# Seven adaLN modulation chunks of a two-layer diffusion step: weighted row sums on VectorE, TensorE only sums over partitions

## The reference

```python
def ada_modulation(cond, w, b):
    mod = jax.nn.silu(cond) @ w + b          # cond: 1024, w: 1024 x 6144
    return [m[:, None, :] for m in jnp.split(mod, 6, axis=-1)]

def modulate(h, shift, scale):
    return h * (1.0 + scale) + shift

# per layer: shift, scale, gate of the mixer, then of the experts
h = modulate(rmsnorm(x, norm_mix[layer]), sh_a, sc_a)
q, k, v = jnp.split(h @ nat_w_qkv[j], 3, axis=-1)      # layer 1
out = neighbourhood_attention(q, k, v, k_cache, v_cache, rpb) @ nat_w_o[j]
x = x + g_a * out
h = modulate(rmsnorm(x, norm_ffn[layer]), sh_f, sc_f)
x = x + g_f * grouped_moe(h, ...)
```

## Time and profile before

| what | value |
|---|---|
| median of 3 runs | 1315.08 us (1310.66 to 1315.25) |
| the profiled execution, whole | 1315.46 us |
| its span, first to last instruction | 1313.6 us |
| granted TensorE clock, mean over the span | 0.989 of full |
| busy: TensorE / VectorE / ScalarE / GpSimd | 1249.4 / 592.7 / 332.7 / 222.7 us |
| modulation matmuls (line 804), all | 1536 instructions, 64 a chunk |
| loads of modulation chunks by SyncE | 24, 2048 KB each |

### The profile page before, as it was taken

The page is one execution under the profiler, slowest core; times in us unless marked ns, Lnnn a source line. Parts: engine busy times, 40 slices in busy tenths (PEclk is TensorE's granted clock), DMA queues, the critical chain, the costliest instruction groups (busy, mean ns, idle before and its releaser), DMA issues.

```text
span 1313.6 us, 20008 instructions
## 1 busy us (share of the span) xinstructions
PE 1249.4 (95%) x7839; PEld 722.0 (55%) x7839; DVE 592.7 (45%) x1514; ACT 332.7 (25%) x785; POOL 222.7 (17%) x298
## 2 busy tenths in 40 slices
PE   5899999999999999999989999999999998999995
PEld 3665466666645654444444455555885455444442
DVE  5221266556535664444452000002883666444446
ACT  4121355445412400000032000002882340000002
POOL 6220500100100012122220100013221001222220
PEclk8999999999999999999989999999999999999998
DMA  9612411221574469999880363135326336999966
GB/s 382 222 41 81 175 66 66 80 116 66 209 270 170 161 240 374 377 375 381 326 262 16 141 229 129 65 142 195 92 58 245 146 129 246 376 378 378 375 182 192
DMA packets 45453, 267.87 MB, mean 204 GB/s; under 512 B 6980, under 2 KB 13460, under 8 KB 31520
## 3 DMA queue, kind: packets, MB, share of 16 engines
q1 hardware_dynamic: 22672, 192.85, 37.6%
q0 software_dynamic: 16928, 52.77, 14.3%
q10 hardware_dynamic: 5760, 20.97, 4.1%
HBM read 230.19 MB, written 34.81 MB: 202 GB/s over the span
## 4 chain that ended last, share of the span: by engine, by line
PE 85%; DVE 5%; DMA 5%; issue 3%; ACT 2%; POOL 0%; POOLq 0%; ACTq 0%; SPq 0%; DVEq 0%
PE PS L1175 14%; PE PS L915 13%; PE PS L1281 11%; PE PS L1129 10%; PE PS L1192 7%; PE PS L782 5%; PE PS L1046 5%; PE PS L788 4%; PE PS L1086 3%; PE PS L804 3%; PE PS L1340 2%; DMA xrows<-big 2%; PE PS L996 2%; PE PS L1303 1%; DMA big<-hrows,big 1%
## 5 line engine op out<-in xcount | busy, mean ns | idle before, releaser
L1129 PE MATMUL PS<-weights,ht 128*128 128x512 f32 x320 | 142.4, 596 | 1.0 <-DVE ht L1683 1.0
L1281 PE MATMUL PS<-ht,weights 128*128 128x128 f32 (+1 forms) x512 | 139.8, 434 | 0.0
L915 PE MATMUL PS<-weights,ht 128*128 128x336 f32 (+1 forms) x320 | 116.7, 523 | 1.6 <-ACT ht L1465 1.6
L1175 PE MATMUL PS<-big 128*128 128x512 f32 x256 | 113.1, 593 | 0.5 <-DVE big L2137 0.5
L1281 PEld LDWEIGHTS PS<-ht,weights 128*128 128x128 f32 x512 | 77.7, 191 | 62.1 <-issue 62.1
L782 PEld LDWEIGHTS PS<-const,big 128*128 128x128 f32 (+2 forms) x627 | 77.0, 144 | 58.1 <-issue 39.6
L782 PE MATMUL PS<-const,big 128*128 128x128 f32 (+2 forms) x627 | 92.3, 283 | 13.6 <-DVE big L1759 4.2
L1593 ACT ACTIVATE big<-PS 128x256 f32<-128x256 f32 x34 | 13.0, 383 | 337.1 <-PE PS L1175 337.1
L1129 PEld LDWEIGHTS PS<-weights,ht 128*128 128x128 f32 x320 | 59.0, 190 | 68.2 <-issue 68.2
L915 PEld LDWEIGHTS PS<-weights,ht 128*128 128x128 f32 x320 | 60.5, 191 | 52.8 <-issue 38.7
L1175 PE MATMUL PS<-weights,big 128*128 128x512 f32 x192 | 84.4, 592 | 0.0
(11 more groups left out here) (256 smaller groups left out, 1817.1 us busy)
## 6 DMA issues: line engine op xcount, KB each, us to landing
weights<-in_ada SPq DMA_DIRECT2D x22, 2048.0 KB, 8.7
big<-in_gu SPq DMA_DIRECT2D x16, 2048.0 KB, 22.7
weights<-in_gu SPq DMA_DIRECT2D x12, 2048.0 KB, 24.2
rows<-in_down SPq DMA_DIRECT2D x18, 1024.0 KB, 12.0
weights<-in_down SPq DMA_DIRECT2D x16, 1024.0 KB
ht<-in_gu SPq DMA_DIRECT2D x6, 2048.0 KB, 24.0
weights<-in_qkv SPq DMA_DIRECT2D x6, 2048.0 KB, 10.7
weights<-in_wo SPq DMA_DIRECT2D x4, 2048.0 KB, 8.9
```

The lines of the kernel that those rows point to most:

```text
L915: ins = pe.matmul(bank(4 + u % 2, n), lhs(k), rhs(k), start=(k == 0), stop=(k == ks - 1))
L1129: ins = pe.matmul(bank(4 + j), OT[:, k, t * P:(t + 1) * P], w[j][:, k, :], start=(k == 0), stop=(k == KD - 1))
L1175: ins = pe.matmul(bank(0), gatT[:, k, :], w[:, k, :], start=(k == 0), stop=(k == KD - 1))
L1281: ins = pe.matmul(bank(bb, n1 - n0), w[:, k, m * P:(m + 1) * P], hT[:, k, n0:n1], start=(k == 0), stop=(k == KD - 1))
```

## The change

Chunks 5 to 11 of the second layer are computed in another way. VectorE reads the chunk's weights (`ada_sums`): for each block k and each of the two conditioning vectors c it multiplies the 128 x 512 block by the per-partition scalar `condT[:, 2k+c]` and adds it to accumulator `acc[c]` (two places of 512 columns in `R`). That is 2 tensor_scalar and 14 scalar_tensor_tensor a chunk; each counts `m_acc`, and each waits for the operation before the last one. TensorE (`ada_summed`) then sums over the partitions: for both c and four groups a product with a two-column selector of constants (`C_PICK`), 8 products where there were 32. The buffer of a chunk's weights is free when VectorE has finished, no longer when TensorE has.

ScalarE takes all evictions of the v units from the second on, of the transposed keys and of the q/k units; VectorE keeps v unit 1. The places of the chunks move: 5 and 6 after v units 5 and 8, 7 to 11 after q/k units 2, 4, 6, 9 and 11. The order of the loads follows. All seven chunks use weight buffer 0. The bias tables come behind the eighth load (n == 7), which is chunk 7.

```diff
--- before.py
+++ after.py
...
@@ -102,6 +103,7 @@
     c[:, C_I16:C_I16 + E] = np.arange(E)
     c[:, C_E128:C_E128 + E] = np.arange(E) * P
     c[:, C_X9:C_X9 + XTILES] = np.arange(XTILES)
+    c[:, C_PICK:C_PICK + 3] = [1, 0, 1]
     c[:, C_EPS] = EPS
     c[:, C_EVEN:C_EVEN + 4] = [2, 4, 6, 8]
     c[:, C_FREE:C_FREE + 5] = [11, 15, 17, 19, 21]
@@ -194,6 +196,7 @@
         Pm = [[R[:, 3456 + (2 * i + j) * 640:3456 + (2 * i + j + 1) * 640] for j in range(2)] for i in range(2)]
         PTm = [R[:, 0:1408], rt[:, 0:1408]]
         ckc = R[:, 5376:5632]
+        acc = [R[:, 4864 + c * 512:4864 + (c + 1) * 512] for c in range(2)]
         ropet = rt[:, 0:1024].rearrange("p (n h x i) -> p n h x i", n=4, h=H, x=2)
 
         qT = big(0, 5120, KD)
@@ -288,6 +291,7 @@
         r_ab = sem("rows_in")
         r_g = sem("gates_in")
 
+        m_acc = sem("ada_sums_on_dve")
         m_mm, m_b, m_cp, m_st, m_tr, m_md = (sem(f"ada_{n}") for n in ("products", "bias_in", "rows", "stored", "transposed", "columns"))
         w_in = [sem(f"w_in{i}") for i in range(5)]
         w_half = sem("w_in3_second_half")
@@ -295,7 +299,7 @@
         g_mm, g_ea, g_ed = (sem(f"products_{x}") for x in ("done", "taken_act", "taken_dve"))
         AT_MM = {"win": 0, "uq": 10, "wo0": 42, "vproj": 52, "wo1": 62}
         AT_EA = {"win": 0, "uq": 5, "vproj": 21}
-        AT_ED = {"win": 0, "uq": 5, "wo0": 21, "vproj": 31, "wo1": 36}
+        AT_ED = {"win": 0, "uq": 5, "wo0": 21, "vproj": 31, "wo1": 32}
         l_sd, l_rs, l_n, l_tr, l_ta, l_td, l_rope, l_qr, k_rc = (sem(n) for n in (
             "lat_sqrt", "lat_rstd", "lat_normed", "lat_transposed", "lat_T_act", "lat_T_dve",
             "k_rope_ready", "q_rope_ready", "krope_copied"))
@@ -305,7 +309,7 @@
         ORDER = (CTX, 0, 1, 2, 3)
         NW = H // 2 * NT
         QK = tuple(range(8, 16)) + tuple(range(8))
-        ADA_QK = (3, 6, 9, 12)
+        ADA_QK = (2, 4, 6, 9, 11)
         WIN = ((0, 0), (1, 0), (0, 1), (1, 1), (2, 0), (2, 1), (3, 0), (3, 1), (4, 0), (4, 1))
         PV = 512 + 256
 
...
@@ -342,11 +346,11 @@
         FRONT = (0, 2, 1, 3)
         LOADS = [[("ada", 0, j) for j in FRONT] + [("win", 0, 0), ("win", 0, 1), ("uq", 0, 0), ("uq", 0, 1), ("ukv", 0, 0)]
                  + [("ada", 0, j) for j in range(4, 12)] + [("wo0", 0, 0), ("wo0", 0, 1)] + [("ada", 1, j) for j in range(4)],
-                 [("ada", 1, 4), ("qkv", 0, 4), ("qkv", 0, 5), ("ada", 1, 5), ("ada", 1, 6), ("ada", 1, 7)] + [("qkv", 0, 2), ("qkv", 0, 3)]
-                 + [("ada", 1, 8), ("ada", 1, 9), ("qkv", 0, 0), ("ada", 1, 10), ("ada", 1, 11), ("qkv", 0, 1), ("wo1", 0, 0), ("wo1", 0, 1)]]
+                 [("ada", 1, 4), ("qkv", 0, 4), ("qkv", 0, 5), ("ada", 1, 5), ("ada", 1, 6), ("qkv", 0, 2), ("qkv", 0, 3), ("ada", 1, 7), ("ada", 1, 8),
+                  ("qkv", 0, 0), ("ada", 1, 9), ("ada", 1, 10), ("qkv", 0, 1), ("ada", 1, 11), ("wo1", 0, 0), ("wo1", 0, 1)]]
 
         SLOTS_ = [[0, 1, 2, 3, 0, 1, 2, 0, 2] + [0, 1] * 4 + [0, 1] + [2] * 4,
-                  [4, 1, 2, 0, 0, 0, 1, 2, 0, 0, 1, 0, 0, 2, 0, 2]]
+                  [4, 1, 2, 0, 0, 1, 2, 0, 0, 1, 0, 0, 2, 0, 0, 2]]
 
         def in_columns(i):
 
@@ -389,6 +393,8 @@
 
         def products_done(what, l, j):
 
+            if what == "ada" and l and j > 4:
+                return m_acc, 16 * (j - 4)
             if what == "ada":
                 return m_mm, l * 12 + (FRONT.index(j) if l * 12 + j < 4 else j) + 1
             if what == "ukv":
@@ -551,7 +557,7 @@
                     sp.wait_ge(c_in[2], 16)
                     for n in range(2, len(LOADS[1])):
                         static_load(1, n)
-                        if n == 8:
+                        if n == 7:
                             sp.wait_ge(s_toepd, 16)
                             sp.wait_ge(c_in[NT - 1], 16)
                             sp.wait_ge(c_sum, 1)
...
@@ -805,6 +810,18 @@
                                         w[:, k, g * P:(g + 1) * P], start=(k == 0), stop=(k == KD - 1))
                 ins.then_inc(m_mm, 1)
 
+            def ada_summed(j):
+
+                i = 12 + j
+                pe.wait_ge(m_cp, i - 1)
+                pe.wait_ge(m_acc, 16 * (i - 16))
+                for c in range(2):
+                    pick = const[:, C_PICK + c:C_PICK + c + 2]
+                    for g in range(4):
+                        ins = pe.matmul(PS[32 * g:32 * g + 2, ada_out_at(i):ada_out_at(i) + P], pick,
+                                        acc[c][:, g * P:(g + 1) * P], start=(c == 0), stop=(c == 1))
+                ins.then_inc(m_mm, 1)
+
             def mod_transpose(i):
 
                 pe.wait_ge(m_cp, i + 1)
@@ -906,7 +923,9 @@
 
             def gemm_unit(name, u, n, ks, lhs, rhs, done=None):
 
-                if u >= 2:
+                if name == "vproj" and u >= 4:
+                    pe.wait_ge(g_ea, AT_EA[name] + u - 2)
+                elif u >= 2:
                     if u % 2 == 0:
                         pe.wait_ge(g_ea, AT_EA[name] + u // 2)
                     else:
@@ -1258,8 +1277,8 @@
                     x_transposes("m1", u + 2)
                 if u == 0:
                     last_part(0, 4)
-                if u in (5, 7, 9):
-                    ada(1, 5 + (5, 7, 9).index(u))
+                if u in (5, 8):
+                    ada_summed(5 + (5, 8).index(u))
 
             pe.wait_ge(kc_in, 32)
             for c in range(KD):
@@ -1271,9 +1290,8 @@
                     w = w_(w_wait(pe, "qkv", 0, u // 4), KD, 512)
                 if n == 1:
                     pe.wait_ge(kc_ta, 1)
-                    pe.wait_ge(kc_td, 1)
                 if n >= 2:
-                    pe.wait_ge(qk_ea if n % 2 == 0 else qk_ed, n // 2)
+                    pe.wait_ge(qk_ea, n - 1)
                 b = (2, 0)[n % 2]
                 m = u % 4
                 for n0, n1, bb in ((0, 512, b), (512, 640, b + 1)):
@@ -1281,10 +1299,9 @@
                         ins = pe.matmul(bank(bb, n1 - n0), w[:, k, m * P:(m + 1) * P], hT[:, k, n0:n1], start=(k == 0), stop=(k == KD - 1))
                 ins.then_inc(qk_mm, 1)
                 if n in ADA_QK:
-                    ada(1, 8 + ADA_QK.index(n))
+                    ada_summed(7 + ADA_QK.index(n))
                 if n == 8:
-                    pe.wait_ge(qk_ea, 4)
-                    pe.wait_ge(qk_ed, 4)
+                    pe.wait_ge(qk_ea, 8)
                     for c in range(KD):
                         ins = transpose(bank(4, P, c * P), kT[:, c, 512:640])
                     ins.then_inc(kc_tr, 1)
...
@@ -1621,7 +1636,7 @@
             def v_out(u):
                 act.wait_ge(g_mm, AT_MM["vproj"] + u + 1)
                 t, j = WIN[u]
-                act.activation(nv[:, t, j * 512:(j + 1) * 512], bank(4), ACT.Copy).then_inc(g_ea, 1)
+                act.activation(nv[:, t, j * 512:(j + 1) * 512], bank(4 + u % 2), ACT.Copy).then_inc(g_ea, 1)
 
             for t in range(NT + 1):
                 if t < NT:
@@ -1636,18 +1651,18 @@
                     ins.then_inc(n_ta, 1)
                 if t == 3:
                     v_out(0)
-            for u in (2, 4, 6, 8):
+            for u in range(2, 10):
                 v_out(u)
             act.wait_ge(kc_tr, 1)
-            act.activation(kcT[:, 0:4, :], bank(0).rearrange("p (c n) -> p c n", c=4), ACT.Copy).then_inc(kc_ta, 1)
-            for n in range(0, 16, 2):
+            act.activation(kcT[:, :, :], bank(0, D).rearrange("p (c n) -> p c n", c=KD), ACT.Copy).then_inc(kc_ta, 1)
+            for n in range(16):
                 act.wait_ge(qk_mm, n + 1)
                 u = QK[n]
                 dst = qT[:, u, :] if u < 8 else kT[:, u - 8, :]
-                act.activation(dst, bank(2, 640), ACT.Copy, scale=-NAT_SCALE if u < 8 else 1.0).then_inc(qk_ea, 1)
+                act.activation(dst, bank((2, 0)[n % 2], 640), ACT.Copy, scale=-NAT_SCALE if u < 8 else 1.0).then_inc(qk_ea, 1)
                 if n == 8:
                     act.wait_ge(kc_tr, 2)
-                    act.activation(kout[:, 0:512], bank(4), ACT.Copy).then_inc(kc_ta, 1)
+                    act.activation(kout, bank(4, D), ACT.Copy).then_inc(kc_ta, 1)
 
             warm(ACT.Exp)
             for w in range(NW + 2):
@@ -1727,6 +1742,20 @@
                     gain = vecT[:, at + 16 + k0:at + 20 + k0].unsqueeze(1).to_broadcast([P, 2, 4])
                     ins = dve.scalar_tensor_tensor(out=dst, in0=dst, scalar=1.0, in1=gain, op0=ALU.add, op1=ALU.mult)
                 ins.then_inc(m_md, 1)
+
+            def ada_sums(i):
+
+                w = w_(w_wait(dve, "ada", 1, i - 12), KD, 512)
+                dve.wait_ge(m_mm, i)
+                for k in range(KD):
+                    for c in range(2):
+                        n = 16 * (i - 17) + 2 * k + c
+                        by = condT[:, 2 * k + c:2 * k + c + 1]
+                        if k == 0:
+                            dve.tensor_scalar(acc[c], w[:, k, :], by, None, ALU.mult).then_inc(m_acc, 1)
```

(44 more changed lines are left out.)

## The result

The changed kernel takes 1304.8 us (median of 5 runs, 1304.3 to 1307.2) against 1315.1 (5 runs, 1310.7 to 1317.2): ratio 0.9929, 95% interval 0.9912 to 0.9946. A second series gave 1307.2 (7 runs, 1303.4 to 1309.5) against 1314.0 (19 runs, 1310.6 to 1316.8): 0.9943, interval 0.9923 to 0.9963. The profiled execution of the changed kernel took 1304.30 us with a span of 1302.4; before it was 1315.46 and 1313.6.

A forecast was written before the change was run, and what follows sets the result against it. TensorE, busy throughout the changed stage, was taken as the bound. Saving 9.1 us, plus 0.5 for stalls and 0.5 for the exp table, gave -8.1 us from a median of 1315.1: forecast 1307.0, range 1303.5 to 1312.5.

The forecast's parts named there:

- TensorE's saving: Chunks 5 to 11 on TensorE: each falls from 1.86 to 0.56 us, seven save 9.1 us.
- rival (2): Stall and exp table cost nothing and a chunk takes TensorE 0.47 us: -9.7, 1305.4 us; chance 0.13.
- The sums: VectorE's 16 operations a chunk: 10.2 us, each starting 0.08 us before the previous one ends.
- The timetable: Loads and sums through weight slot 0: ready before TensorE asks, slack 1.4, 0.9 and 0.3 us at chunks 7 to 9.
- The turn to slower at 15.4: Chunk sums lasting 15.4 us or more would make the kernel slower than before by 0.5%.
- 3S - 30.9: Stall in us by chunk 9, with S the time of a chunk's sums; none at S = 10.2.
- The first q/k weights: Load after v unit 8: 7.7 us, 0.65 us to spare, or 0.6 late if it takes 8.9.
- The charge of 0.5 for all stalls: 0.5 us charged for chunk stalls up to chunk 9 and the first q/k weights together.
- The exp table: Attention's start: ScalarE's table load follows its last eviction and delays the first exp, +0.5 us (0 to 0.6).
- The sum: Whole kernel: -9.1 + 0.5 + 0.5 = -8.1 us, giving 1307.0 us.
- (1): Loop of load and sums through weight slot 0 binds, TensorE waits: 1308.5 to 1313.5 us; chance 0.28.
- (3): VectorE's sums slow down on SBUF access shared with another engine; kernel slower, about 1335 at doubled operations; chance 0.04.

The follow-up runs named there:

- the run with the closer wait: Changed kernel, but each VectorE sum waits for the operation just before it, not the one before that: 1310.9 us, ratio 0.9969.
- the evictions on VectorE: Changed kernel without ScalarE's part: VectorE keeps every second eviction, placed between its sums: 1304.6 us, ratio 0.9918.
- the run with the evictions alone: Kernel before with only the evictions moved to ScalarE, chunks as before: 1315.1 us against 1314.0, ratio 1.0006.

## Why the prediction was right

The forecast was 1307.0, with -8.1 us. The stage gave -7.65, and both measured medians lie inside the range. The main step held: a chunk takes TensorE 0.55 us instead of 1.86, and VectorE's sums are ready in time. Some of the agreement is luck, for two errors in the timetable cancelled and the costs around it came out otherwise than charged.

- **TensorE's saving.** 0.56 us a chunk was taken from the router's logit parts; it is 0.55. Seven times 1.86 - 0.55 is 9.2. The scaled 0.47 of rival (2) is wrong: a chunk of a quarter of the instructions costs 0.3 of the time. By the drain of the Trainium skill (TensorEngine Tiling (Array Packing), Key Properties) a fixed part was to be expected, and 0.55 - 0.47 = 0.08 us is room for one, though the runs don't show what it consists of.
- **The sums.** 10.2 forecast, 10.15 measured. The tensor_scalar takes 0.48, not 0.5. The spacing was the choice that mattered, and the earlier trace rows had both cases: 0.79 where the result before is needed, as in the run with the closer wait, and a start 0.08 before the end where it isn't, as in the changed kernel (0.66 for 0.745). The rule of the Trainium skill (VectorE: DVE Perf Modes, The DRAIN you can't avoid) is that the next operation does not start until the pipeline is empty, but the section adds that one that is not held starts earlier, an exception that the prediction left out. The trace fits the first with the closer wait, where the next start lies 0.04 us after the end, and the second in the changed kernel, where it lies 0.08 before it.
- **The timetable.** Chunks 7, 8 and 9 were given slacks of 1.4, 0.9 and 0.3; they were 4.3, 4.0 and 1.7. The term that was off is the load of chunk 7: I pieced 14.8 us together, it took 13.0 (13.3 with the evictions on VectorE). The 2.4 us for the bias tables behind it were too much; the row that they came from was one of a scatter, for the load that took 13.3 us in the earlier trace rows took 11.6 in the run with the evictions alone. Partly the later q/k units helped too, being 0.85 us late themselves. The next two loads, put at 8.0 each, took 8.2 and 10.1, and 17.5 to 18.6 together in all eight profiles with the new places. With the forecast's 14.8 for chunk 7's load the 1.7 us of chunk 9 would have been used up, and without the late q/k units as well it would have been some 1 us late (my estimate from these figures). So two errors cancelled. The form of the loop is right: from the measured slacks it gave 3.2 us for the closer wait (2.9 of waiting). The turn to slower at 15.4 (0.54% at 15.5) agrees in its total only: the prediction's 3S - 30.9 makes 15.6 us of waiting there, and 11.3 were measured, with 3.8 of lower clock that it had no term for.
- **The first q/k weights.** 0.65 us to spare was forecast, from one row with 7.7 us; the load took 9.3 and 9.6, and TensorE waited 0.85 and 1.23. The step named the danger (0.6 late at 8.9) but its upper end was too low. The charge of 0.5 for all stalls was 0.3 to 0.7 too small.
- **The exp table.** +0.5 forecast, +0.37 measured by the evictions alone at the second scores, and by the first products of probabilities and values 0.2, or 0.7 to 0.9 where the clock fell. The clock was no term of the prediction. The first exp came 2.13 us after the last unit, 0.35 later than before and not 0.6; I had put the table at the right place but let the first exp wait for the whole of the dummy one, which it overlaps by 0.1 (901.44 + 0.20 against 901.55).
- **The sum.** 9.2 - 0.85 - 0.37 = 8.0 against 7.65 in the first pair; the missing 0.3 or so is what the q/k units take longer with a fifth chunk among them, a term that the prediction didn't have. The medians differ by 10.3 us in the first series and by 6.8 in the second, since the stretches outside the stage scatter; the prediction had that as a width only and not as a mechanism.
- **The rivals.** (1) did not happen at S = 10.15 and did at 11.9. (3) came only by adding operations: the 98 sums last 0.741 to 0.749 us, so VectorE wasn't slowed by another engine in this stage, although both operands of each lie in SBUF. The sharing that the Trainium skill tells of (GPSIMD Engine Reference, Specifications) was hardly tried: GpSimd issued only its four small DMAs a chunk, and in the first profile these fell beside the sums of chunks 6 and 11 alone, for 2.3 us each, without slowing them. A GpSimd that computes beside the sums was not measured.

## What to carry to other kernels

Work that leaves the bounding engine pays one for one only as long as the new chain keeps its timetable: write down, for each place where the bounding engine asks for a result, load, landing, work and free, and find the period of that loop; here 10.15 + 8.2 to 10.1 us a round against 18.05, so each round spends reserve, and the 4.3 us in hand at chunk 7 were 1.7 at chunk 9. A step of the same shape elsewhere in the trace (the router's 16 matmuls) is a better price than a proportion. Compare two executions between the same instructions, for a total can move by more than the change does, and put the last mark far enough behind the change: two profiles of the changed kernel differ by 0.4 us up to the second scores and by 1.1 a few products later.

## What the runs showed of the hardware

- An idle time of TensorE can cost more than its length. Behind 6.81 us the granted clock was 0.50 (1.2 GHz) and 2.1 us more were lost; behind 3.40, 1.7 more; behind 2.35 us, at chunk 9 of the kernel with the closer wait, the clock stayed at 1.00. At the reload single waits of 3.0 and 3.4 us went with a clock of 0.50, and 1.6 to 1.9 us followed by 0.90 and 0.4 with 1.00 three times; but once 1.97 and 0.90 went with the lower clock as well, and so did a single 2.12. At the attention's start 0.79 and 1.16 us with 1.2 us of work between them went with 0.50 in six profiles and with 1.00 in two, one of these of the same kernel as one of the six. The idle time alone does not decide it, and where the border lies is open.
- VectorE operations of 128x512 that wait for the one just before start 0.79 us apart; with the wait on the one before that, 0.66. A semaphore count and wait on every operation shows no cost in itself: the sums start 0.08 us before the end of the one before, as the tensor_scalars of the same chunk do, which wait for none of their neighbours.
